# Three stages that gather five columns in places of their own before the norm factor, with a norm statistic of one product

## The reference, cut to what matters

```python
def rmsnorm_2(x, g):
    y = xf * lax.rsqrt(jnp.mean(xf * xf, axis=-1, keepdims=True) + EPS)
    return y * g
def sq_relu_mlp(h, w_up, w_down):              # w_up 1024 x 4096, w_down 4096 x 1024
    return jnp.square(jax.nn.relu(h @ w_up)) @ w_down
for layer in range(2):
    h = rmsnorm_2(x, mix_norm[layer])
    y = mixer_ab(h, ...) if layer % 2 == 0 else mixer_c(h, ...)
    x = x + y
    x = x + sq_relu_mlp(rmsnorm_2(x, mlp_norm[layer]), w_up[layer], w_down[layer])
```

## Time and profile before

| | |
|---|---|
| time, median of three runs | 866.03 us (864.93 to 867.61) |
| the profiled execution's own time | 865.05 us |
| its span, first to last instruction | 863.1 us |
| TensorE busy, matmuls | 851.2 us, 99%, 7296 matmuls |
| VectorE / ScalarE / GpSimd busy | 607.3 / 469.7 / 95.2 us |
| mean granted TensorE clock | 0.998 |
| HBM read | 148.14 MB, 173 GB/s over the span |

### The profile page before, as it was taken

How to read it: one execution, slowest core, us unless ns; L and a number is a source line. 1 busy time by engine, 2 the same in 40 slices (tenths; PEclk the granted TensorE clock), 3 DMA queues, 4 the chain that set the end, 5 groups by cost and what they waited for, 6 DMA issues and landing times.

```text
span 863.1 us, 19328 instructions
## 1 busy us (share of the span) xinstructions
PE 851.2 (99%) x7296; PEld 818.0 (95%) x7296; DVE 607.3 (70%) x997; ACT 469.7 (54%) x754; POOL 95.2 (11%) x148
## 2 busy tenths in 40 slices
PE   9999999999999999999999999999999999999996
PEld 8988899999999999788999999999999999999996
DVE  5776567666666687877876666668979966666665
ACT  5646766444434485448654444446786744444443
POOL 4320002000000039510100000002110100000001
PEclk9999999999999999999999999999999999999999
DMA  7533246565565648624465565654544566555551
GB/s 257 172 123 98 98 147 224 196 210 183 186 205 184 197 160 234 177 97 140 167 207 194 194 194 194 194 194 148 172 147 153 168 218 193 194 189 190 188 187 49
DMA packets 44291, 151.61 MB, mean 176 GB/s; under 512 B 5589, under 2 KB 6869, under 8 KB 44245
## 3 DMA queue, kind: packets, MB, share of 16 engines
q1 hardware_dynamic: 41040, 145.00, 51.3%
q0 software_dynamic: 2400, 4.89, 1.8%
q10 hardware_dynamic: 804, 1.06, 0.4%
HBM read 148.14 MB, written 1.05 MB: 173 GB/s over the span
## 4 chain that ended last, share of the span: by engine, by line
PE 88%; DVE 6%; ACT 3%; issue 1%; POOL 1%; DMA 1%; SPq 0%; DVEq 0%; POOLq 0%; ACTq 0%
PE bank L1424 26%; PE bank L1425 26%; PE bank L1426 26%; DVE alo L995 2%; PE bank L1820 1%; DVE wlo L970 1%; PE bank L1454 1%; PE bank L1446 1%; PE bank L1591 1%; PE bank L1568 1%; PE bank L1910 1%; PE bank L1539 1%; DVE h L1008 1%; DMA raw<-in_slabs 1%; ACT whi L550 1%
## 5 line engine op out<-in xcount | busy, mean ns | idle before, releaser
L1424 PE MATMUL bank<-ahi,whi 128*128 128x256 f32 (+1 forms) x1392 | 394.7, 284 | 0.7 <-DVE alo L988 0.5
L1426 PE MATMUL bank<-ahi,wlo 128*128 128x256 f32 (+1 forms) x1392 | 386.8, 278 | 0.0
L1425 PE MATMUL bank<-alo,whi 128*128 128x256 f32 (+1 forms) x1392 | 386.6, 278 | 0.0
L970 DVE TENSOR_TENSOR wlo<-raw,whi 128x1024 fp32r<-128x1024 f32 x272 | 331.3, 1226 | 25.8 <-ACT whi L550 25.8
L550 ACT ACTIVATE whi<-raw 128x1024 fp32r<-128x1024 f32 x272 | 281.4, 1051 | 84.9 <-PE bank L1426 76.2
L1424 PEld LDWEIGHTS bank<-ahi,whi 128*128 128x128 f32 x1392 | 261.9, 188 | 5.6 <-DVE alo L988 2.4
L1425 PEld LDWEIGHTS bank<-alo,whi 128*128 128x128 f32 x1392 | 261.6, 188 | 0.4
L1426 PEld LDWEIGHTS bank<-ahi,wlo 128*128 128x128 f32 x1392 | 261.6, 188 | 0.0
L1424 PE MATMUL bank<-hidhi,whi 128*128 128x256 f32 x704 | 194.5, 276 | 0.6 <-DVE wlo L970 0.6
L1426 PE MATMUL bank<-hidhi,wlo 128*128 128x256 f32 x704 | 194.4, 276 | 0.0
L1425 PE MATMUL bank<-hidlo,whi 128*128 128x256 f32 x704 | 194.3, 276 | 0.0
(11 more groups left out here) (234 smaller groups left out, 725.8 us busy)
## 6 DMA issues: line engine op xcount, KB each, us to landing
raw<-in_slabs SPq DMA_DIRECT2D x272, 512.0 KB, 3.5
shared<-in_convw POOLq DMA_DIRECT2D x4, 512.0 KB, 6.7
shared<-zpad POOLq DMA_DIRECT2D x48, 35.5 KB, 3.8
raw<-in_slabs SPq DMA_DIRECT2D x8, 128.0 KB, 5.5
vtok<-in_gatew POOLq DMA_DIRECT2D x2, 512.0 KB, 4.8
out<-y SPq DMA_DIRECT2D x4, 256.0 KB, 2.3
h<-in_xT ACTq DMA_DIRECT2D x3, 272.0 KB, 5.7
h<-in_xT SPq DMA_DIRECT2D x1, 272.0 KB, 3.8
```

What stands on the lines that cost most here:

```text
L970: dve.tensor_tensor(wlo[:, n % R, :, :], raw[:, n % R, :, :], whi[:, n % R, :, :].bitcast(F32), ALU.subtract).then_inc(lo_done, 1)
L1424: pe.matmul(dst, hi, xh, start=start, stop=False, skip_group_check=True)
L1425: pe.matmul(dst, hi, xl, start=False, stop=False, skip_group_check=True)
L1426: return pe.matmul(dst, lo, xh, start=False, stop=stop, skip_group_check=True)
```

## The change

The three stages are IN2, MLP2 and MLP3 (norms `N_MIX0`, `N_MLP0`, `N_MLPC`). Five columns are gathered before any evacuation, each in its own PSUM place (`late_place`: half of the statistic's bank, the two gemm banks, two halves of the auxiliary bank). The statistic goes to the other half of its bank, as one product in column 4 (the fifth), behind its first chunk. GpSimd adds all eight squares to one (`all_sum`: four sums of two and three chained adds), from the moment VectorE has split the third column's slab. In the MLPs ScalarE squares behind all eight high parts. Splits of slabs n+4 to n+6 move ahead of the norm factor on ScalarE and VectorE. In the MLPs rows 0 to 3 follow the five columns, and the slabs' order in memory with them. In IN2 the plain squares' statistic moves behind column 6, and ScalarE's plain squares ahead of the factor.

```diff
+FIRST_SPLITS = {1: (4,), 2: (5, 6), 3: (7,), 4: (8,)}
-PLAIN_COLUMN = 4
+PLAIN_COLUMN = 6
+SQUARES_LAST = {7: (0, 2, 4, 6)}
-SUMS = ((0, 2, 4, 6), (0, 2, 4, 6), (0, 6), (0, 2, 4, 6), (0, 6), (0, 2, 4, 6))
+SUMS = ((0, 2, 4, 6), (0, 2, 4, 6), (0,), (0,), (0, 6), (0,))
+LATE = {N_MIX0: IN2, N_MLP0: MLP2, N_MLPC: MLP3}
+LATE_COLUMNS = 5
+        def late_place(i):
+            if i < LATE_COLUMNS:
+                return (half(stat_bank, 0), gemm_bank[0][:, NMETA:T1], gemm_bank[1][:, NMETA:T1], half(aux_bank, 0),
+                        half(aux_bank, 1))[i]
+            return gemm_bank[i % 2][:, NMETA:T1]
+        def relu_buf(f):
+            return f if f < LATE_COLUMNS - 1 else hid_buf(f, FF2 - 1)
...
+            def all_sum(i):                                     # GpSimd
+                pool.wait_ge(lo_done, LATE[i] + 3)
+                for a in (0, 2, 4, 6):
+                    pool.wait_ge(sq_ready, KC * i + a + 2)
+                    n[0] += 1
+                    pool.tensor_tensor(sq[:, a, NMETA:], sq[:, a, NMETA:], sq[:, a + 1, NMETA:], ALU.add).then_inc(pool_chain, 1)
+                pool.wait_ge(pool_chain, n[0])
+                add_chunk(i, 0, 2)
+                add_chunk(i, 4, 6)
+                add_chunk(i, 0, 4, sum_ready)
-            six_and_two(N_MIX0)
+            all_sum(N_MIX0)
...
-            pair_sums(N_MLP0)
+            all_sum(N_MLP0)
...
             split_early(IN2)                                    # ScalarE
-            act.wait_ge(stat_ready, N_MIX0 + 1)
-            inverse_root(rstd[:, NMETA:], std[:, NMETA:], half(stat_bank, 0), DM, eps2).then_inc(rstd_ready, 1)
+            split_ahead(IN2 + 2)
+            split_ahead(IN2 + 3)
             for k in range(0, KC, 2):
                 act.activation(t8[:, k:k + 2, :], h[:, k:k + 2, NMETA:], ACT.Square).then_inc(plain_sq, 2)
+            act.wait_ge(stat_ready, N_MIX0 + 1)
+            inverse_root(rstd[:, NMETA:], std[:, NMETA:], stat_place(N_MIX0), DM, eps2).then_inc(rstd_ready, 1)
...
             split_early(MLP2)                                   # ScalarE, MLP3 alike
-            norm_factor(N_MLP0, stat_bank[:, 0:SEQ])
+            split_ahead(MLP2 + 2)
+            split_ahead(MLP2 + 3)
+            norm_factor(N_MLP0, stat_place(N_MLP0))
...
             split_early(MLP2)                                   # VectorE, IN2 and MLP3 alike
+            for i in range(1, 4):
+                split_ahead(MLP2 + i)
             dve.wait_ge(rstd_ready, RS0[N_MLP0] + 1)
...
             def squared_relu_mlp(base, e0, m0):                 # VectorE
-                for f in range(3):
+                for f in range(LATE_COLUMNS):
                     squared_relu(f, base + f, e0, m0)
-                split_ahead(base + 4)
+                    for n in FIRST_SPLITS.get(f, ()):
+                        split_ahead(base + n)
...
+            def late_columns(n, i):                             # TensorE
+                for c in range(2, LATE_COLUMNS):
+                    column(n + c, None, place=late_place(c), amid=(lambda: stats(i)) if c == LATE_COLUMNS - 1 else None, at=1)
...
             first_columns(IN2, A_MIX0)
-            stats(N_MIX0)
-            for i in range(2, len(IN2_FIRST)):
-                if i > 2:
-                    pe.wait_ge(gemm_evac, E_IN2 + i - 1)
-                column(IN2 + i, col_bank(i))
+            late_columns(IN2, N_MIX0)
+            for i in range(LATE_COLUMNS, len(IN2_FIRST)):
+                pe.wait_ge(gemm_evac, E_IN2 + (3 if i < 7 else i - 1))
+                column(IN2 + i, None, place=late_place(i))
                 if i == PLAIN_COLUMN:
                     plain_stats()
...
                 first_columns(base, s)                          # TensorE, the MLPs
-                stats(i)
-                column(base + 2, col_bank(2))
-                hidden_row(0, base + 3, m0, first=True, acc=acc)
-                hidden_row(1, base + 4, m0 + 1, acc=acc)
+                late_columns(base, i)
+                for f in range(LATE_COLUMNS - 1):
+                    hidden_row(f, base + LATE_COLUMNS + f, m0 + f, first=(f == 0), acc=acc, buf=relu_buf(f))
```

More of the change, by code:

```diff
@@ L213, in col_bank, with first_place, stat_place @@
             return aux_bank if i == 2 else gemm_bank[i % 2]
+        def late_place(i):
[3 more added lines that the diff above has]
+            return gemm_bank[i % 2][:, NMETA:T1]
+        def first_place(s, b, lo):
+            return late_place(b) if s in (A_MIX0, A_MLP0, A_MLPC) else gemm_bank[b][:, lo:T1]
+        def stat_place(i):
+            return half(stat_bank, 1 if i in LATE else 0)
         def in1_bank(i):
@@ L578, in residual_hi @@
                         act.activation(chunk(ahi, k, lo), h[:, k, lo:], ACT.Copy, scale=par[:, g:g + 1]).then_inc(ahi_ready, 1)
-                        for j in (SQUARES_CHUNKS if i in (N_MIX0, N_MIXC) else SQUARES_ROWS).get(k, ()):
+                        order = SQUARES_CHUNKS if i in (N_MIX0, N_MIXC) else SQUARES_LAST if i in LATE else SQUARES_ROWS
+                        for j in order.get(k, ()):
                             residual_squares(i, j)
@@ L1012, in acc_add, with take @@
                         residual_lo(i, s, j)
-            def take(n, src, d, scale=1.0, lo=NMETA, ahead=True):
+            def take(n, src, d, scale=1.0, lo=NMETA, ahead=True, place=None):
                 dve.wait_ge(slab_used, n + 1)
-                dve.scalar_tensor_tensor(proj[:, d, lo:], src[:, lo:T1], scale, rstd[:, lo:],
+                dve.scalar_tensor_tensor(proj[:, d, lo:], src[:, lo:T1] if place is None else place, scale, rstd[:, lo:],
                                          ALU.mult, ALU.mult).then_inc(gemm_evac, 1)
@@ L1212, in _ @@
             split_early(IN2)
+            for i in range(1, 4):
+                split_ahead(IN2 + i)
             dve.wait_ge(rstd_ready, RS0[N_MIX0] + 1)
@@ L1242, in _ @@
             for i, c in enumerate(IN2_FIRST):
-                take(IN2 + i, col_bank(i), c, QSCALE if 8 <= c < 12 else 1.0)
+                if i == 3:
+                    dve.wait_ge(slab_used, IN2 + LATE_COLUMNS)
+                take(IN2 + i, None, c, QSCALE if 8 <= c < 12 else 1.0, ahead=i > 3, place=late_place(i))
                 tap = taps(tap, TAPS_COLUMN.get(i, 0))
@@ L1299, in _ @@
             split_early(MLP2)
+            for i in range(1, 4):
+                split_ahead(MLP2 + i)
             dve.wait_ge(rstd_ready, RS0[N_MLP0] + 1)
             def squared_relu(f, n, e0, m0, q=0, row=True):
-                dve.wait_ge(slab_used, n + 1 + 4 * q)
-                dve.scalar_tensor_tensor(hid[:, f % 2, :], col_bank(f)[:, NMETA:T1], 0.0, rstd[:, NMETA:],
+                dve.wait_ge(slab_used, n + 1 + 4 * q + (1 if f == 3 else 0))
+                dve.scalar_tensor_tensor(hid[:, f % 2, :], late_place(f), 0.0, rstd[:, NMETA:],
                                          ALU.max, ALU.mult).then_inc(gemm_evac, 1)
-                split_ahead(n, q)
+                if f >= LATE_COLUMNS:
+                    split_ahead(n, q)
                 dve.wait_ge(gemm_evac, e0 + f + 1 + 2 * q)
@@ L1312, in squared_relu @@
                 dve.wait_ge(hid_hi, m0 + f + 1 + 2 * q)
-                b = hid_buf(f, FF2 - 1)
+                b = relu_buf(f)
                 dve.tensor_tensor(hidlo[:, b, :], hid2[:, f % 2, :], hidhi[:, b, :].bitcast(F32),
                                   ALU.subtract).then_inc(hid_lo, 1)
-                if f >= 2 and row:
+                if f >= LATE_COLUMNS and row:
                     split_ahead(n + 1, q)
             def squared_relu_mlp(base, e0, m0):
-                for f in range(3):
+                for f in range(LATE_COLUMNS):
                     squared_relu(f, base + f, e0, m0)
-                split_ahead(base + 4)
-                with dve.Fori(0, (FF2 - 5) // 2) as it:
+                    for n in FIRST_SPLITS.get(f, ()):
+                        split_ahead(base + n)
+                with dve.Fori(0, (FF2 - 7) // 2) as it:
                     for j in range(2):
-                        squared_relu(3 + j, base + 5 + 2 * j, e0, m0, it)
+                        squared_relu(LATE_COLUMNS + j, base + 9 + 2 * j, e0, m0, it)
                 squared_relu(FF2 - 3, base + 2 * FF2 - 7, e0, m0)
@@ L1402, in _ @@
             split_early(MLP3)
+            for i in range(1, 4):
+                split_ahead(MLP3 + i)
             dve.wait_ge(rstd_ready, RS0[N_MLPC] + 1)
@@ L1429, in slab_ready, with column @@
                 pe.wait_ge(lo_done, n + 1 + R * q)
-            def column(n, bank, q=0, lo=NMETA, amid=None, in1=False):
+            def column(n, bank, q=0, lo=NMETA, amid=None, in1=False, place=None, at=3):
                 slab_ready(n, q)
                 for k in range(KC):
-                    if amid and k == 3:
+                    if amid and k == at:
                         amid()
```

(13 more changed lines are left out.)

33 lines of the change are left out of this document (18 added, 15 removed).

## The result

The changed kernel takes 875.58 us (median of 6 runs, 874.15 to 877.0) against 865.43 us before (6 runs): ratio 1.0119, 95% interval 1.0108 to 1.0129. It is slower, by 10.15 us where 6.5 were forecast, and 3.1 us above the 872.5 on record (the kernel before measures 0.6 lower here than the 866.03 it started from). The profiled execution took 876.51 us, span 874.8.

The account below looks back on a forecast made before the run. TensorE, busy in 99% of the span, was taken as the bound. Two MLPs at +2.3 us and IN2 at +1.9 gave +6.5: 865.05 to 871.55, plus 0.98 to the median, so 872.5 us; 8 in 10 for 865 to 877.

Parts of the forecast that it names:

- High and low parts, column 2: All three stages: column 2 starts earlier, 2.2 us per MLP with low parts 0.40 us apart, 1.48 us in IN2.
- The collision: GpSimd's adds meet four queued VectorE splits in each stage; the late sum makes TensorE wait 3.3 us in column 4.
- In turns: Adds and splits alternate: an add ends 0.60 us after the split ahead, a split 1.08 after the add ahead.
- t1: Moment VectorE has split column 2's slab and GpSimd starts adding; 426.04 in the first MLP, sum forecast at t1 + 9.25.
- the clock falls in the wait: Rival: each halt brings an equally long stretch at the lower clock, +5 us in all, 877.5 us; chance 0.08.
- Rows 0 and 3: MLP rows behind the five columns: row 0 waits 0.4 us more, row 3 0.3 us, for VectorE's work.
- The cover in IN2 for the convolution's copies: GpSimd's later copies still land about a microsecond ahead of their products: cost nothing, or 0.5 us if cover is gone.

Follow-up runs that it names:

- e1_busy: The changed kernel with thirteen spare products of ones on TensorE ahead of the statistic's product in each of the three stages: 872.41 us.
- e10_shift: The changed kernel with only an unused scratch tile declared ahead of the hidden rows' operands, moving these and later tiles by 64 bytes a partition: 888.04 us.
- e8_halfhalt: e4_tree with its three adds moved behind the three splits and one spare sum ahead of the last add, so VectorE alone halts TensorE: 878.51 us.
- e4_tree: The changed kernel with the seven adds off GpSimd; VectorE sums the squares in three adds between splits n+4 and n+5: 861.91 us.
- e3_early: The changed kernel without GpSimd's wait for column 2's low weights, so it adds as soon as the squares are there: 870.39 us.
- e5_gap: The changed kernel with short scratch writes on VectorE ahead of splits n+4 to n+6, the scratch declared ahead of the hidden rows' operands: 886.08 us.

## Why the prediction was right in direction and short by 3 us

- High and low parts, column 2: right. Eight low parts in 3.25 us (forecast 3.2); column 2 2.18 us earlier against the first high part (2.2), in IN2 1.44 (1.48).
- The collision: the size was right, the form in one stage of three. "In turns" was read from the earlier trace rows, which are of IN2, and in IN2 it held: the sum came at t1 + 9.2 (9.25). In the two MLPs the first add waited out the whole run of splits, and the sum came at t1 + 9.5. TensorE waited 3.08 us in IN2, and 3.37 and 3.29 in the MLPs (3.3). That both forms make the sum nearly equally late (four adds in 6.69 and in 6.99 us) was luck for the forecast. What decides between them no run shows: e1_busy and e10_shift repeat it stage for stage.
- The step that failed is the one that gave the halt no price beyond its length. The prediction had it as a rival, "the clock falls in the wait", at 0.08, because the earlier trace rows showed a fall only where TensorE had nothing left to do. e1_busy puts it at 3.2 us for three stages (the rival said 5), e8_halfhalt shows that it needs no GpSimd. Forecast 872.5 plus 3.2 is 875.7, and 875.58 was measured; by differences it fits less closely, 6.5 plus 3.2 is 9.7 against 10.15. The Trainium skill, "TensorE: Matmul & The Clock Gate", section "HAM oscillation — how this bites in real kernels", was the better guide here: waits between bursts put the array back to half rate, and the trace agrees (0.51 behind a 3.37 us halt). The rival deserved more than its 0.08.
- Rows 0 and 3: priced at 0.4 and 0.3, and right where the sum is in time. In e4_tree's first MLP row 0's first product starts 0.33 us behind the one ahead of it and its second 0.22 later, where 0.11 is usual: 0.33 us in all; row 3 loses 0.29 in the same way. In e1_busy row 0 loses 0.25; in the changed kernel, where slow products stand ahead of row 0, no such step is seen.

```profile
434.30 0.28 PE L1493 MATMUL bank<-ahi,wlo 128*128 128x256 f32 x1
434.63 0.38 PE L1491 MATMUL bank<-hidhi,whi 128*128 128x256 f32 x1
434.85 0.28 PE L1492 MATMUL bank<-hidlo,whi 128*128 128x256 f32 x1
```

- The cover in IN2 for the convolution's copies, which I took at nothing, held in the changed kernel; with the clock kept up (e1_busy) the products waited 0.7 us for the copies, near the 0.5 that I had named for it.

## What to carry to other kernels

Before work is moved to an idle engine, list what runs beside it in its new place. Here seven adds of 0.74 us were late because VectorE had a row of splits queued at that very moment, and three adds on the busy engine itself were in time. Price a halt of TensorE amid dense work as its length and a slow stretch behind it; where a halt of some three microseconds can't be avoided, spare products in it cost less than the clock. A part of a change can owe its gain to another part: the columns with the old statistic lost 3.6 us, with the one product and its sum in time the whole won 3.3.

## What the runs showed of the hardware that I had not expected

- A GpSimd add begun inside a run of VectorE splits without gaps was held until the run's end in both MLPs of the changed kernel (3.92 and 3.93 us, 0.74 alone), and for 6.68 us, into the first gap, in e3_early's second. In IN2 the same add, begun inside a split in the same way, got in as that split ended, and the two alternated, about 1.7 us a pair. A write of 0.06 us between splits made them alternate in the MLPs too. The Trainium skill, "SBUF — State Buffer", section "Who interferes with whom", says that an operation of VectorE with two SBUF inputs contends with GpSimd's reads; the trace agrees, and adds that back-to-back splits lose nothing in it while they hold GpSimd off (1.14 us apart). What decides between the two forms is open, as it is for the low parts in e3_early.
- The clock's fall is not certain at this length: in e5_gap's first MLP a halt of 3.06 us was followed by a granted clock of 1.00, in its second one of 3.06 us by 0.69.

```profile
442.00:446.00 4.00, 3.95 (x33) 3.73 (x32) 2.39 (x6) 2.19 (x5) 0.00 (x0) 1.00 0.08 30
...
705.00:709.00 4.00, 3.89 (x22) 3.84 (x23) 2.04 (x5) 1.74 (x5) 0.05 (x1) 0.69 0.18 70
```

- Moving the hidden rows' operands by 64 bytes a partition slowed those products: they start 0.120 us apart, and no longer 0.113.
